# Zero fill of the expert slots: issued behind the first norm instead of behind the last gate unit

## The chip, the cores and the metric

The kernel runs on one core of one Trainium2 chip. The metric is device microseconds (us) from the first to the last instruction of one execution with what lies around it; less is better. The engines are named as the profile names them: PE (TensorE, matrix multiplies), DVE (VectorE), ACT (ScalarE), POOL (GpSimd) and SP (SyncE, which here only issues DMAs). All of them run at once and wait for each other through semaphores.

## What is computed

The reference is one inference step of a two-layer backbone over 640 tokens of 1024 channels, 128 context tokens and 512 latent ones. Each layer is a mixer and a mixture of experts, each behind a norm that is scaled and shifted:

```python
for l in range(DEPTH):                       # DEPTH = 2
    sh1, sc1, gt1, sh2, sc2, gt2 = ada_modulation(cvec, w_mod[l], b_mod[l])
    h = rmsnorm(x, norm_mix_g[l]) * (1.0 + sc1) + sh1
    y = mixer_ab(h, ...) if l % 2 == 0 else mixer_c(h, ...)
    x = x + gt1 * y
    h = rmsnorm(x, norm_ffn_g[l]) * (1.0 + sc2) + sh2
    x = x + gt2 * moe_ffn(h, router, bias, w1[l], w3[l], w2[l])
```

The mixer of layer 0 projects `h` to seven parts. Two feed a gated linear recurrence (RG-LRU: `xr`, `yr`, with gates from small block matrices), five feed a chunked recurrence with matrix states (HGRN2: `q`, two forget gates, `v`, `og`). In the mixture of experts each token goes to 2 of 16 experts:

```python
combine = jnp.sum(one_hot(idx, N_EXPERTS) * wsel[..., None], axis=1)   # 2 of 16 per token
hid = silu(einsum('md,edf->mef', hf, w1)) * einsum('md,edf->mef', hf, w3)
return einsum('mef,efd->md', hid * combine[..., None], w2)
```

## The kernel before, in words

Activations lie with channels on the 128 partitions, eight blocks of 128 channels by 640 tokens. The program of each engine is written out by hand in one block per engine; every engine takes its own list in order.

PE writes its results into a ring of four tiles in PSUM. `tile_plan` (function `T`) numbers all tiles in the order in which PE fills them; `psum_full` counts finished tiles, so a wait for `psum_full` at `T["name"] + n` is a wait until PE has finished the n-th tile of that name. Weights come through a ring of three slots of 1 MB. SP's `load_until` (line 568) issues the loads in a fixed order, and load i waits until PE has finished the last tile that uses load i − 3. PE waits for a load on `w_landed`.

Layer 0 begins on PE like this: transposes of the input, eight pieces of modulation (`mod0a`), the sums of the first norm (tile `norm0`), four `xr` and four `yr` projection tiles (two tiles for each 1 MB load of `ab_w_in`), and then eight units u = 0 to 7. A unit is two gate tiles (`gate`, from the small gate matrices `GW`) and one projection tile (`qk`). Behind each odd unit stand four further pieces of modulation (`mod0b`, one 1 MB load of `w_mod` each, 16 matmuls each) and a tile of transposes. Behind unit 7 follow the projections `kb`, `v` and `og`, and then the levels of the chunked recurrence. The norm's root is taken by ACT (lines 1399, 1400), the multiply by DVE (line 1789), scale and shift by ACT (line 1410), and `xr` starts on the first scaled blocks.

The mixture of experts sends tokens by their expert: a slot array in device memory, `slots_in` (`expert_inputs` in the trace), has 25 blocks of 128 rows, one for each of 16 experts and 9 for the overflow; `slots_out` (`expert_outputs`) has the same shape. Rows that no token fills are read too, so `slots_in` is filled with zeros, and so are the 9 overflow blocks of `slots_out`. The source is `ZERO`, 128 x 1024 zeros in SBUF, so each of the 34 fills moves 512 KB. POOL issues them in lines 723 to 726, and POOL waits for all of them (`zero_filled`) at the head of its part of the first mixture of experts, before it scatters tokens.

POOL's own list at the start is: small vectors, the gate matrices, the router, the memset of `ZERO`, then a wait for the second gate tile of unit 7 (`T["gate7"] + 2`). That wait protects `SIN`, the place of the recurrence's starting state, which lies in the second half of `GW`; the load of `state_hgrn` into it is issued next, and the 34 fills behind it. Then POOL takes its multiplies in the levels of the chunked recurrence (lines 737, 738).

Of the kernel before, what the change touches and what calls it, by code (L numbers as in the profile page):

```python
# [15 lines left out]
P = 128  # L16
# [149 lines left out]
def build(nc, A, const, outs, xspill, slots_in, slots_out):  # L166
# [6 lines left out]
    T = tile_plan()  # L173
    VB = vec_places()
    ctx = ExitStack()
    with ctx:  # L176
# [3 lines left out]
        def sem(name):  # L180
            return ctx.enter_context(nc.semaphore(name))
# [65 lines left out]
        psum_full = sem("psum_full")  # L247
# [91 lines left out]
        for i in range(4):  # L339
            add(("rw_wo", i), T["wo"] + 2 * i + 1, cols(A["rw_wo"][0], 256 * i, 256))  # L340
        slot_no = {key: i for i, (key, _, _) in enumerate(stream)}
        landed_at, per_slot = [], [0] * RING_W
        for i, (_, _, parts) in enumerate(stream):
            per_slot[i % RING_W] += 16 * len(parts)
            landed_at.append(per_slot[i % RING_W])
# [40 lines left out]
        SIN = GW[:, 8 * P:16 * P]  # L386
# [304 lines left out]
        def _(pool):  # L691
# [13 lines left out]
            for wi, name in enumerate(("rg_wa", "rg_wx")):  # L705
                for d in range(2):
                    src = A[name][0, d].rearrange("(c b) i j -> b i c j", b=2)
                    for b in range(2):
# [7 lines left out]
            pool.dma_start(rbias, rb.to_broadcast([P, NE])).then_inc(S["router_in"], 16)  # L716
            nc.gpsimd.memset(ZERO, 0.0).then_inc(S["zero_ready"], 1)

            pool.wait_ge(psum_full, T["gate7"] + 2)
            pool.dma_start(SIN.rearrange("p (j v) -> p j v", v=P),  # L720
                           A["state_hgrn"][0, 0].rearrange("d h k v -> k (d h) v")).then_inc(S["st_in"], 16)
            pool.wait_ge(S["zero_ready"], 1)
            for e in range(NE + N_OVER):
                pool.dma_start(slots_in[e * P:(e + 1) * P, :], ZERO).then_inc(S["zero_filled"], 16)
            for e in range(NE, NE + N_OVER):
                pool.dma_start(slots_out[e * P:(e + 1) * P, :], ZERO).then_inc(S["zero_filled"], 16)

            for h in range(NH_A):
                for lv in range(LEVELS):
                    i = h * LEVELS + lv  # L730
                    s = 1 << lv
                    nb = NT // (2 * s)
                    ek = EK[i % 3].rearrange("p (n two s) -> p n two s", two=2, s=s)
                    kf = K[0][:, h, :].rearrange("p (n two s) -> p n two s", two=2, s=s)
                    kb = K[1][:, h, :].rearrange("p (n two s) -> p n two s", two=2, s=s)
                    pool.wait_ge(S["lvl_exp"], 2 * i + 2)
                    nc.gpsimd.tensor_tensor(ek[:, :, 0, :], ek[:, :, 0, :], kf[:, :, 0, :], ALU.mult)
                    nc.gpsimd.tensor_tensor(ek[:, :, 1, :], ek[:, :, 1, :], kb[:, :, 1, :],
                                            ALU.mult).then_inc(S["lvl_k"], 1)
# [1798 lines left out]
```

## Time and profile before

| | us |
|---|---|
| median of 3 runs | 2493.36 |
| lowest and highest of them | 2492.8, 2500.39 |
| profiled execution | 2489.1 |
| its span, first to last instruction | 2487.3 |
| PE busy in it | 2086.2 (84%) |
| DVE, ACT, POOL busy | 974.9, 701.6, 376.7 |
| mean granted clock of PE | 0.894 |

All rows further down are of the one profiled execution, and times in them count from the start of its span. Busy shares are means over many stages with different limits, so a stage is read by itself: by what its engines wait for, by the granted clock of PE (1.00 is full speed) and by the share of the 16 DMA engines and the GB/s that they move. For a DMA the trace gives the time at which an engine issued it and the time until it landed.

### The profile page before, as it was taken

What the parts mean: (1) busy time and instruction counts of PE and PEld (TensorE: products, weight loads), DVE (VectorE), ACT (ScalarE), POOL (GpSimd) and SP (SyncE); (2) the same over time, 40 slices, a digit from 0 to 9 for tenths busy, and PEclk for the clock granted to TensorE, in tenths of its full rate; (3) what the DMA queues carried; (4) which work ended last, traced back from release to release, by engine and by line L of the source; (5) the groups of instructions that cost most, each with busy time, mean ns of one, the idle gap of its engine ahead of it and who ended that gap; (6) DMA issues with size and microseconds to landing.
All of it is one profiled execution on the core that took longest, in us unless ns stands there. A gap on an engine that the chain in (4) does not pass through costs nothing. (4 is left out here: it accounts for less than half of the span.)

```text
span 2487.3 us, 35375 instructions
## 1 busy us (share of the span) xinstructions
PE 2086.2 (84%) x14628; PEld 1519.2 (61%) x14628; DVE 974.9 (39%) x2165; ACT 701.6 (28%) x1491; POOL 376.7 (15%) x870
## 2 busy tenths in 40 slices
PE   6999698777885999559998998888888879759993
PEld 3454365444544777335577887878877865647762
DVE  2236303566222111271124566665666551311104
ACT  1245213222121111130034555444544330301112
POOL 3000300333001000200013333133223300010001
PEclk9999899898995999779999898886888899679996
DMA  8134832333224899622122111211121221469963
GB/s 277 34 119 135 310 138 68 104 115 122 92 89 165 272 342 343 200 92 69 51 61 48 34 42 42 44 33 35 40 42 33 52 77 35 152 220 344 344 232 136
DMA packets 330272, 322.30 MB, mean 130 GB/s; under 512 B 119028, under 2 KB 299488, under 8 KB 329728
## 3 DMA queue, kind: packets, MB, share of 16 engines
q1 hardware_dynamic: 311200, 253.70, 33.0%
q0 software_dynamic: 17456, 60.55, 6.4%
q10 hardware_dynamic: 1456, 5.77, 0.6%
q8 instruction: 118, 1.93, 0.3%
q14 instruction: 42, 0.34, 0.0%
HBM read 252.86 MB, written 67.12 MB: 129 GB/s over the span
## 5 line engine op out<-in xcount | busy, mean ns | idle before, releaser
L831 PE MATMUL psum_ring<-arena 64*64 64x32 f32 (+6 forms) x4800 | 625.6, 316 | 62.7 <-DVE arena L2311 28.6
L831 PEld LDWEIGHTS psum_ring<-arena 64*64 64x64 f32 (+2 forms) x4800 | 464.8, 179 | 183.8 <-issue 105.3
L831 PE MATMUL psum_ring<-arena,weight_ring 128*128 128x128 f32 (+2 forms) x1680 | 346.2, 359 | 6.1 <-DVE arena L2105 3.4
L831 PEld LDWEIGHTS psum_ring<-arena,weight_ring 128*128 128x128 f32 x1680 | 239.2, 198 | 110.8 <-issue 102.8
L831 PE MATMUL psum_ring<-h_normed,weight_ring 128*128 128x512 f32 (+1 forms) x768 | 214.9, 442 | 11.4 <-ACT h_normed L1410 5.8
L831 PE MATMUL psum_ring<-weight_ring,arena 64*64 64x64 f32 (+4 forms) x1776 | 195.4, 292 | 17.1 <-DVE h_normed L2381 4.1
L831 PE MATMUL psum_ring<-weight_ring,small 128*2 128x256 f32 x768 | 178.2, 390 | 18.0 <-DMA weight_ring<-in_w_mod 17.6
L831 PEld LDWEIGHTS psum_ring<-weight_ring,arena 64*64 64x64 f32 (+2 forms) x1776 | 170.6, 173 | 34.3 <-issue 10.3
L831 PEld LDWEIGHTS psum_ring<-h_normed,weight_ring 128*128 128x128 f32 x768 | 119.4, 195 | 106.1 <-issue 100.4
L831 PEld LDWEIGHTS psum_ring<-weight_ring,small 128*2 128x2 f32 x768 | 64.0, 86 | 121.2 <-DMA weight_ring<-in_w_mod 18.7
L1912 DVE COPY arena<-psum_ring 128x1024 f32<-128x1024 f32 x36 | 44.1, 1225 | 180.7 <-PE psum_ring L915 180.6
L831 PE MATMUL psum_ring<-x_resid,weight_ring 128*128 128x512 f32 (+1 forms) x320 | 88.9, 440 | 25.7 <-DVE x_resid L2175 25.7
L1435 ACT ACTIVATE arena<-psum_ring 128x256 f32<-128x256 f32 x36 | 13.8, 383 | 324.0 <-PE psum_ring L831 324.0
L1920 DVE TENSOR_TENSOR arena<-arena,psum_ring 128x256 f32<-128x256 f32 x36 | 15.2, 422 | 229.5 <-ACT arena L1435 229.5
L915 PE MATMUL psum_ring<-consts,arena 128*128 128x128 f32 x360 | 54.1, 285 | 53.5 <-DMA arena<-expert_inputs 53.5
L915 PEld LDWEIGHTS psum_ring<-consts,arena 128*128 128x128 f32 x360 | 46.7, 149 | 74.2 <-DMA arena<-expert_inputs 53.7
L831 PEld LDWEIGHTS psum_ring<-x_resid,weight_ring 128*128 128x128 f32 x320 | 49.4, 194 | 65.1 <-issue 65.1
L752 POOL DMA_DIRECT2D expert_outputs<-arena x36 | 19.3, 537 | 444.7 <-ACT arena L1430 427.6
L1394 ACT ACTIVATE h_normed<-x_resid 128x640 f32<-128x640 f32 x40 | 28.7, 734 | 200.5 <-DVE x_resid L1808 194.5
L797 POOL COPY arena<-arena 32x256 f32<-32x256 f32 x20 | 12.1, 603 | 463.1 <-DMA arena<-expert_outputs 463.1
L806 POOL TENSOR_TENSOR arena<-arena 64x14 f32<-64x14 f32 (+6 forms) x280 | 78.3, 279 | 21.9
L804 POOL TENSOR_TENSOR arena<-arena 64x14 f32<-64x14 f32 (+6 forms) x280 | 76.2, 272 | 22.0
(384 smaller groups left out, 2799.2 us busy)
## 6 DMA issues: line engine op xcount, KB each, us to landing
arena<-in_moe_w SPq DMA_DIRECT2D x108, 1024.0 KB, 10.5
weight_ring<-in_w_mod SPq DMA_DIRECT2D x48, 1024.0 KB, 5.1
expert_outputs<-arena POOLq DMA_DIRECT2D x45, 512.0 KB, 7.8
arena<-expert_inputs SPq DMA_DIRECT2D x36, 512.0 KB, 7.5
weight_ring<-in_ab_w_in SPq DMA_DIRECT2D x14, 1024.0 KB, 5.0
expert_inputs<-arena POOLq DMA_DIRECT2D x25, 512.0 KB, 17.4
arena<-expert_outputs SPq DMA_DIRECT2D x80, 128.0 KB, 3.2
expert_outputs<-arena SPq DMA_DIRECT2D x26, 256.0 KB, 2.8
```

The costliest lines, as they stand in the source:

```text
L752: pool.dma_start(slots_out[e * P:(e + 1) * P, :], YB[e % 2]).then_inc(y_stored[e % 2], 16)
L797: link(nc.gpsimd.tensor_copy(square(triL[0:NB_T]), turned(triX[0:NB_T])))
L804: link(nc.gpsimd.tensor_tensor(prod, l3[:, k + 1:, k:k + 1].broadcast_to([2 * NB_T, m, k]), r3[:, k:k + 1, 0:k].broadcast_to([2 * NB_T, m, ...
L806: link(nc.gpsimd.tensor_tensor(r3[:, k + 1:, 0:k], r3[:, k + 1:, 0:k], prod, ALU.subtract))
L831: return nc.tensor.matmul(out, lhsT, rhs, start=start, stop=stop)
L915: ins = nc.tensor.transpose(ps[:, k * P:(k + 1) * P], src[:, k * P:(k + 1) * P], ident)
L1394: A_(H[:, k, :], X[:, k, :], ACT.Square).then_inc(S["sq_ready"], 1)
L1435: A_(SH[e % 2], ps[:, 0:DE], ACT.Silu).then_inc(S["silu_out"], 1)
L1912: free(nc.vector.tensor_copy(XGT[e % 2], ps), n)
L1920: free(TT(HM[e % 2], SH[e % 2], tile(n)[:, 512:512 + DE], ALU.mult), n)
```

## The change

The load of `state_hgrn` with its wait for `T["gate7"] + 2` moves from ahead of the 34 fills to behind them. The fills get a wait of their own, for the tile `norm0`, with which PE has finished the sums of the first norm. The wait for `zero_ready` (the memset of `ZERO`) stays with the fills. The number of DMAs, their sizes and the queue that they are issued on are as before.

```diff
@@ -716,15 +716,16 @@
             pool.dma_start(rbias, rb.to_broadcast([P, NE])).then_inc(S["router_in"], 16)
             nc.gpsimd.memset(ZERO, 0.0).then_inc(S["zero_ready"], 1)
 
-            pool.wait_ge(psum_full, T["gate7"] + 2)
-            pool.dma_start(SIN.rearrange("p (j v) -> p j v", v=P),
-                           A["state_hgrn"][0, 0].rearrange("d h k v -> k (d h) v")).then_inc(S["st_in"], 16)
             pool.wait_ge(S["zero_ready"], 1)
+            pool.wait_ge(psum_full, T["norm0"] + 1)
             for e in range(NE + N_OVER):
                 pool.dma_start(slots_in[e * P:(e + 1) * P, :], ZERO).then_inc(S["zero_filled"], 16)
             for e in range(NE, NE + N_OVER):
                 pool.dma_start(slots_out[e * P:(e + 1) * P, :], ZERO).then_inc(S["zero_filled"], 16)
 
+            pool.wait_ge(psum_full, T["gate7"] + 2)
+            pool.dma_start(SIN.rearrange("p (j v) -> p j v", v=P),
+                           A["state_hgrn"][0, 0].rearrange("d h k v -> k (d h) v")).then_inc(S["st_in"], 16)
             for h in range(NH_A):
                 for lv in range(LEVELS):
                     i = h * LEVELS + lv
```

POOL's list at this place before, with the semaphores that a row waits for (`in_state_hgrn` is the state, `expert_inputs` and `expert_outputs` are the two slot arrays):

```order
L717 MEMSET arena 128x1024
L720 DMA arena<-in_state_hgrn 128x8x128 [waits psum_full]
L724 DMA expert_inputs<-arena 128x1024 [waits zero_ready]
L724 DMA expert_inputs<-arena 128x1024 x24
L726 DMA expert_outputs<-arena 128x1024 x9
L737 ISA
L737 TENSOR_TENSOR h_normed<-h_normed,arena 128x320 [waits lvl_exp]
```

Here the wait for the gate tiles (`psum_full` in the row of L720) stands ahead of all the fills. POOL's list at the same place in the changed kernel, whose lines from there on are numbered anew:

```order
L717 MEMSET arena 128x1024
L722 DMA expert_inputs<-arena 128x1024 [waits psum_full,zero_ready]
L722 DMA expert_inputs<-arena 128x1024 x24
L724 DMA expert_outputs<-arena 128x1024 x9
L727 DMA arena<-in_state_hgrn 128x8x128 [waits psum_full]
L738 ISA
L738 TENSOR_TENSOR h_normed<-h_normed,arena 128x320 [waits lvl_exp]
```

The 34 fills have moved ahead of the state's load, behind an earlier wait (`psum_full` of `norm0`); the wait for the gate tiles now holds the state's load alone. The lists of the other engines, SP's weight loads among them, are the same in both kernels.

## Rows read from the trace of the kernel before

**Rows 1.** The page's slices of 62.2 us: memory traffic.
```profile
GB/s 277 34 119 135 310 138 68 104 115 122 92 89 165 272 342 343 200 92 69 51 61 48 34 42 42 44 33 35 40 42 33 52 77 35 152 220 344 344 232 136
```

**Rows 2.** Waits of PE, 274.2 to 330 us: total, times, longest.
```profile
PE psum_ring L831 <- DMA weight_ring<-in_w_mod: 17.6, 2, 11.7
```

**Rows 3.** Timeline of PE, 274.2 to 330 us: start, length, group, idle time before it.
```profile
274.26 7.07 PE L831 MATMUL psum_ring<-weight_ring,small 128*2 128x256 f32 x32
293.00 5.77 PE L831 MATMUL psum_ring<-weight_ring,small 128*2 128x256 f32 x16 [11.67 <-DMA weight_ring<-in_w_mod]
304.76 5.03 PE L831 MATMUL psum_ring<-weight_ring,small 128*2 128x256 f32 x16 [5.98 <-DMA weight_ring<-in_w_mod]
...
316.54 13.84 PE L831 MATMUL psum_ring<-h_normed,weight_ring 128*128 128x512 f32 x41 [5.60 <-DMA weight_ring<-in_ab_w_in]
```

**Rows 4.** Timeline of PE, 230 to 256 us, behind unit 5.
```profile
237.37 13.97 PE L831 MATMUL psum_ring<-weight_ring,small 128*2 128x256 f32 x64
...
252.44 2.43 PE L831 MATMUL psum_ring<-arena 128*128 128x512 f32 x8
```

**Rows 5.** Timeline of POOL, 15 to 290 us, and line 726.
```profile
265.98 0.90 POOL L720 DMA_DIRECT2D arena<-in_state_hgrn  x1 [243.91 <-PE psum_ring L831]
266.87 13.24 POOL L724 DMA_DIRECT2D expert_inputs<-arena  x25
...
L726 POOL DMA_DIRECT2D expert_outputs<-arena x9: 532/532/534, 280.1 to 284.3; - x9
...
DMA to landing us min/median/max: 31.6/36.0/40.7
```

**Rows 6.** Weight loads of line 568, issued 270 to 282 us.
```profile
L568 SPq DMA_DIRECT2D weight_ring<-in_w_mod x2: 368/368/368, 274.4 to 277.9; - x2
L568 SPq DMA_DIRECT2D weight_ring<-in_ab_w_in x1: 8818/8818/8818, 281.4 to 281.4; - x1
...
DMA to landing us min/median/max: 18.6/26.8/35.1
```

**Rows 7.** Weight loads of line 568, issued 90 to 110 us.
```profile
L568 SPq DMA_DIRECT2D weight_ring<-in_ab_w_in x2: 368/368/368, 90.1 to 107.4; - x2
...
DMA to landing us min/median/max: 4.9/4.9/5.0
```

**Rows 8.** Windows: length, busy time (instructions) by engine, granted clock, DMA share, GB/s.
```profile
270.00:281.00 11.00, 11.00 (x49) 4.87 (x47) 8.56 (x7) 6.63 (x8) 11.00 (x22) 1.00 1.02 398
281.00:293.00 12.00, 0.33 (x3) 0.00 (x1) 2.55 (x6) 0.09 (x1) 3.82 (x8) 0.61 1.04 410
322.00:420.00 98.00, 98.00 (x397) 65.93 (x396) 14.96 (x16) 19.45 (x26) 0.00 (x0) 1.00 0.22 74
```

**Rows 9.** Timeline of ACT, 60 to 145 and 320 to 340 us.
```profile
63.95 0.77 ACT L1399 ACTIVATE psum_ring<-psum_ring,consts 128x640 f32<-128x640 f32 x1 [30.38 <-PE psum_ring L831]
...
124.76 0.70 ACT L1466 ACTIVATE arena<-psum_ring 128x640 f32<-128x640 f32 x1 [7.95 <-PE psum_ring L831]
...
142.07 0.70 ACT L1466 ACTIVATE arena<-psum_ring 128x640 f32<-128x640 f32 x1 [7.95 <-PE psum_ring L831]
...
327.82 0.70 ACT L1491 ACTIVATE arena<-psum_ring 128x640 f32<-128x640 f32 x1 [46.74 <-PE psum_ring L831]
...
336.48 0.70 ACT L1491 ACTIVATE arena<-psum_ring 128x640 f32<-128x640 f32 x1 [7.36 <-PE psum_ring L831]
```

**Rows 10.** Timeline of PE, 62 to 146 us.
```profile
69.67 72.36 PE L831 MATMUL psum_ring<-h_normed,weight_ring 128*128 128x512 f32 x256 [5.76 <-ACT h_normed L1410]
141.87 2.33 PE L831 MATMUL psum_ring<-arena 128*128 128x512 f32 x8
```

**Rows 11.** Timeline of DVE: 62 to 75, 232 to 246, 267 to 283 us.
```profile
66.75 5.68 DVE L1789 TENSOR_TENSOR h_normed<-x_resid,psum_ring 128x1280 f32<-128x1280 f32 x4 [5.97 <-ACT psum_ring L1400]
...
236.75 4.15 DVE L2022 RECIPROCAL arena<-arena 128x640 f32<-128x640 f32 x1
...
272.69 4.15 DVE L2022 RECIPROCAL arena<-arena 128x640 f32<-128x640 f32 x1
```

## The prediction

> **What bounds the kernel now.** The page first: the chain of work at its end is spread over PE, ACT, DVE and DMA, so no single engine's share says what this edit is worth. The slices of the page do: where the edit works, in the fifth slice (249 to 311 us), the core moves 310 GB/s while its neighbours move 135 and 138 [rows 1]. Next, what PE waits for there. Between 274 and 330 us its longest are for weight loads, 17.6 us in two waits for `w_mod` [rows 2]. The timeline of PE puts them in order and adds a third: the four `w_mod` pieces behind unit 7 start at 274.26, stall until 293.00 and again until 304.76, and the next projection (`kb`) starts at 316.54, 5.60 us of that a wait for `ab_w_in` [rows 3]. The same stretch of unit 5, with no fill beside it, goes from 237.37 to 252.44 [rows 4]. POOL's timeline names the culprit: 34 fills of 512 KB (25 to `expert_inputs`, 9 to `expert_outputs`) are issued from 266.87, one each 0.53 us, the last at 284.3, and it lands 40.7 us later, at 325.0 [rows 5]. Weight loads issued beside them at 274.4, 277.9 and 281.4 take 18.6, 26.8 and 35.1 us to land [rows 6]; undisturbed ones take 4.9 to 5.0 [rows 7]. They land at 293.0, 304.7 and 316.5, exactly where PE resumes, 11.8 us apart. So this stretch is bound by DMA bandwidth: the windows show the engines at a share of 1.04 and 410 GB/s while PE works 0.33 us of 12 [rows 8]. ACT and DVE only wait for PE there.
>
> **The change part by part.** *(a) The fills leave 266.87 to 325.0.* The weight loads then take 5 us as behind units 1, 3 and 5. The loads issued at 274.4 and 277.9 would land at 279.4 and 282.9, before PE comes to them at 281.2 and 284.7 (two and three pieces of 13.97/4 = 3.49 us behind 274.26 [rows 4]), the one of 281.4 at 286.4, before `kb` at 289.3. The stretch shrinks from 316.54 − 274.26 = 42.28 us to unit 5's 252.44 − 237.37 = 15.07: **27.2 us saved**, waits and half-speed pieces together.
>
> *(b) The clock behind the stall.* PE is idle from 281, the granted clock falls to a mean of 0.61 in 281 to 293 (1.00 is 2.4 GHz, the lower level is 1.2) [rows 8], and the idle stretches before 304.76 and 316.54 repeat it. The first projection of `kb` takes from 316.54 until ACT reads it at 327.82: 11.28 us. Its neighbour takes 336.48 − 327.82 = 8.66 [rows 9], plus 0.20 from PE's next start to ACT's read (141.87 and 142.07 [rows 9, 10]). **2.4 us saved**: with no idle time PE keeps 2.4 GHz, as it does behind unit 5.
>
> *(c) Who is late next.* From 322 to 420 PE is busy 98.00 us of 98 at clock 1.00 [rows 8] with the `kb`, `v` and `og` projections; ACT and DVE wait for PE's tiles, POOL for ACT's exponents. Nothing there has a fixed time, so the whole path moves up. The state load keeps its wait on the last gate unit (265.98 [rows 5]) and now has an empty queue behind it; its reader comes over 100 us later. Cost: nothing.
>
> *(d) The fills arrive behind the first norm.* POOL has been idle since 22 us; it is released when PE ends the sums of `norm0`, 63.95 by ACT's read [rows 9], plus the 0.3 us it took at 265.98. The 34 issues take 18 us on POOL, which nobody waits for. The data: 34 x 0.524 MB = 17.8 MB at 398 to 410 GB/s [rows 8] is 45 us alone, 58.1 us in the old place (266.87 to 325.0) with about four weight loads sharing. Here two loads share, so about 53 us, bounds 45 and 58: it ends near 117 us (109 to 122.4). In the whole of 64 to 125 us SP issues only two loads, at 90.1 and 107.4 [rows 7]. The first belongs to `yr` tile 2, which starts when `yr` tile 1 is done, at 124.6 (ACT's read at 124.76 [rows 9]); the second is needed behind the gate tiles of 141.87 [rows 10]. With 18.6 us (a first load beside the fill [rows 6]) they land at 108.7 and 126.0: 16 us to spare each. With the worst landing seen, 35.1, they are at 125.2 and 142.5, under 1 us late. With the fill ahead of everything until 122.4, the first lands at 127.3, 2.7 us late. Cost 0, bounds 0 and 3; I take 0, because the nearest row, one load in flight beside the fill, is 18.6.
>
> *(e) The fill beside PE, DVE and ACT.* In 270 to 281, with the fill at 398 GB/s, PE is busy 11.00 of 11.00 us at clock 1.00 [rows 8]; DVE's reciprocal takes 4.15 us beside POOL's issues (272.69) and 4.15 without (236.75) [rows 11]. Cost 0. The cover is gone only if the norm's chain on DVE and ACT (64 to 70 us), for which PE waits 5.76 us [rows 10], is different; that is rival 1.
>
> **Sum**: 27.2 + 2.4 = 29.6 us off the profiled execution's 2489.1 (span 2487.3): 2459.5. The median of the runs is 2493.4, 4.3 above it, and the forecast of a median is 2493.4 − 29.6 = **2463.8 us**.
>
> **Rivals.** *1. POOL's burst holds DVE.* The first multiplies of the norm (DVE, 66.75 to 72.4 [rows 11]) would lie inside POOL's 18 us of issues (64.3 to 82.4). If DVE had to wait for the burst's end, PE's first projection would move by 82.4 − 66.75 = 15.6 us: 2479.4. Against it: the equal reciprocals of (e). A page bears on this. The Trainium skill, "SBUF — State Buffer", section "SBUF: two separate sides", says that VectorE and GpSimd share a pair of ports as an exclusive lock, held for a whole instruction, and that a DMA issued from GpSimd needs it to write its descriptors; it limits this to VectorE's two-port modes and to some operations with two SBUF inputs. By that rule the burst might be late as well as DVE; the rows show neither, and the norm's multiply has one operand in PSUM.
>
> *2. The clock does not come back.* If the pieces ran as slowly as beside the stall, only the waits are saved, 11.67 + 5.98 + 5.60 = 23.2 us [rows 3]: 2470.2. Against it: unit 5 has equal work before it, and its pieces take 13.97 us.
>
> *3. The loads were slow for another reason, or the fill does not start early:* 2493. For it speaks only that the profile infers releasers; against it the landing times, which hold to the fill's end. POOL's queue holds nothing ahead of the fills after 22 us.
>
> *4. Slower: the fill outlasts its room.* Place: `yr` tile 2 at 124.6, waiting for the load issued at 90.1. If weight loads got nothing until the fill ends, and it ran slower than in the old place, PE would wait; the gain is used up when that load lands later than 124.6 + 29.6 = 154.2, so when 17.8 MB take from 66 to 149 us, 215 GB/s or less. At the 135 GB/s of the slice ahead of the old place [rows 1] the fill takes 132 us and ends at 198, the load lands at 203, and PE loses 78 us: 2493.4 − 29.6 + 78 = 2542. Against it: the same bytes on the same queue moved at 400 GB/s, and loads beside it did get 1 MB each 11.8 us.
>
> **How the numbers follow.** Forecast 0.88; rival 1: 0.03; rival 2: 0.04; rival 3: 0.03; rival 4: 0.02. A measurement of this kernel tells 0.3% (7.5 us) from no change. Faster holds the forecast and rivals 1 and 2: 0.95; same is rival 3: 0.03; slower 0.02. The range: the runs before lie from 2489.1 to 2500.4, so −4 and +7 about the median; with the 29.6 taken off that is 2459.5 to 2470.8. Cost (d) of up to 3 and rival 2 (2470.2) widen the top to 2474. The two saved terms come from one neighbour each, and a stall less can also shift a later fall of the clock, whose size the spread of the runs gives as some 4 us: the bottom goes to 2455.
>
> **What would show it.** Right: POOL's fills start at about 64.3 us and the last lands between 109 and 122; PE runs from 69.7 to the gates without a wait; the loads of 90.1 and 107.4 land in some 19 us; PE goes from the last `w_mod` pieces at 274 to `kb` at 289, at clock 1.00; `kb`'s first read by ACT is near 298; everything from there is 29.6 us earlier. Wrong: a wait of PE for `in_ab_w_in` near 125, DVE's multiplies of the norm longer than 5.68 us, or new waits between 289 and 400 us that take the place of the old.

## The result

| | us | ratio to before, 95% interval |
|---|---|---|
| before, median of four runs | 2493.08 | |
| changed kernel, median of four runs (2460.35 to 2473.12) | 2465.27 | 0.9888 (0.9853 to 0.9923) |
| changed kernel, measured a second time, median | 2464.74 | 0.9868 (0.9840 to 0.9895) |
| profiled execution, before and after | 2489.1, 2460.35 | |
| its span, before and after | 2487.3, 2458.5 | |

Each ratio is to runs of the kernel before that were made beside it. The changed kernel is faster by 27.8 us by the medians; the forecast was a gain of 29.6 us, to a median of 2463.8. The second measurement was made beside the experiments:

> The changed kernel once more, on the chip of these runs, as the mark for the others: ratio 0.985 to 0.991.

**The stretch behind unit 7.** The timeline of PE in the changed kernel, 262 to 330 us, answers rows 3:

```profile
272.83 13.97 PE L832 MATMUL psum_ring<-weight_ring,small 128*2 128x256 f32 x64
287.32 0.65 PE L870 MATMUL psum_ring<-consts,arena 2*128 2x2 f32 x8 [0.51 <-DVE arena L1770]
287.90 34.88 PE L832 MATMUL psum_ring<-h_normed,weight_ring 128*128 128x512 f32 x128
```

The four `w_mod` pieces run in one block of 13.97 us and `kb` starts at 287.90, 15.07 us after the first of them, as behind unit 5 before [rows 4] and where the kernel before took 42.28. The weight loads issued there (line 568, 270 to 282 us; issue time, then landing) answer rows 6:

```profile
L568 SPq DMA_DIRECT2D weight_ring<-in_w_mod x2: 368/368/368, 272.9 to 276.5; - x2
L568 SPq DMA_DIRECT2D weight_ring<-in_ab_w_in x1: 367/367/367, 279.9 to 279.9; - x1
...
DMA to landing us min/median/max: 5.0/5.1/5.1
```

They land in 5 us in place of 18.6 to 35.1. (On the page the fifth slice of the span now moves 140 GB/s in place of 310 [rows 1], the second 325 in place of 34.) The waits of PE in the whole first 420 us (total, times, longest) are:

```profile
PE psum_ring L996 <- DMA arena<-in_rw_lnb: 17.5, 1, 17.5
PE psum_ring L832 <- POOL h_normed L739: 13.3, 1, 13.3
PE psum_ring L832 <- ACT h_normed L1411: 5.8, 1, 5.8
PE psum_ring L870 <- DVE arena L1770: 3.0, 6, 0.5
```

No wait for a load of `w_mod` or `ab_w_in` is left [rows 2], and none has come up elsewhere. The waits for `in_rw_lnb`, for the norm (line 1411) and for line 1770 were there before with the same 17.5, 5.8 and 3.0 us. The wait for POOL (13.3 us, line 739) is that of line 738 before, at the first level of the chunked recurrence; it had 13.32 us there and has only moved into the window.

**The fills in their new place.** POOL's timeline, 15 to 290 us, and the landing times of the last nine fills answer rows 5:

```profile
64.55 13.12 POOL L722 DMA_DIRECT2D expert_inputs<-arena  x25 [42.47 <-PE psum_ring L832]
77.67 4.72 POOL L724 DMA_DIRECT2D expert_outputs<-arena  x9
264.55 0.91 POOL L727 DMA_DIRECT2D arena<-in_state_hgrn  x1 [182.16 <-PE psum_ring L832]
...
L724 POOL DMA_DIRECT2D expert_outputs<-arena x9: 532/532/534, 77.7 to 81.9; - x9
...
DMA to landing us min/median/max: 26.7/29.9/34.4
```

They are issued from 64.55, the last at 81.9, and it lands 34.4 us later, at 116.3. The two weight loads issued meanwhile answer rows 7 (one window each):

```profile
L568 SPq DMA_DIRECT2D weight_ring<-in_ab_w_in x1: 368/368/368, 88.7 to 88.7; - x1
...
DMA to landing us min/median/max: 18.3/18.3/18.3
...
L568 SPq DMA_DIRECT2D weight_ring<-in_ab_w_in x1: 368/368/368, 106.0 to 106.0; - x1
...
DMA to landing us min/median/max: 11.6/11.6/11.6
```

They land at 107.0 and 117.6; PE comes to the first at about 123.1 (0.20 us ahead of ACT's read at 123.33) and to the second behind 140.44. The windows (columns as in rows 8) and PE's timeline from 62 to 146 us [rows 10]:

```profile
70.00:82.00 12.00, 12.00 (x40) 6.48 (x40) 3.57 (x5) 8.06 (x14) 12.00 (x24) 0.89 1.02 374
82.00:109.00 27.00, 27.00 (x102) 15.05 (x101) 10.12 (x21) 3.93 (x4) 0.39 (x1) 1.00 1.03 401
281.00:293.00 12.00, 11.49 (x53) 5.59 (x52) 2.36 (x7) 0.00 (x0) 0.00 (x0) 1.00 0.81 264
```

```profile
69.70 70.90 PE L832 MATMUL psum_ring<-h_normed,weight_ring 128*128 128x512 f32 x256 [5.76 <-ACT h_normed L1411]
140.44 2.33 PE L832 MATMUL psum_ring<-arena 128*128 128x512 f32 x8
```

With the DMA engines at 374 and 401 GB/s PE is busy in every microsecond of 70 to 109, and the 5.76 us that it waits for the norm are the same to the digit [rows 10]. DVE's multiplies of the norm and ACT's reads of `yr` tile 1 and of the first `kb` tile [rows 9, 11]:

```profile
66.77 5.68 DVE L1790 TENSOR_TENSOR h_normed<-x_resid,psum_ring 128x1280 f32<-128x1280 f32 x4 [5.98 <-ACT psum_ring L1401]
```

```profile
123.33 0.70 ACT L1467 ACTIVATE arena<-psum_ring 128x640 f32<-128x640 f32 x1 [7.95 <-PE psum_ring L832]
...
296.85 0.70 ACT L1492 ACTIVATE arena<-psum_ring 128x640 f32<-128x640 f32 x1 [17.19 <-PE psum_ring L832]
```

The multiplies take 5.68 us beside POOL's burst as they did without it. `kb` is read at 296.85, 30.97 us earlier than at 327.82.

### The profile page after: what moved, and what is told of

The parts are those of the page before. It is cut to its first block and busy times, and to the rows that moved or that the text cites. A ratio compares the mean times of both kernels' runs of the same rounds, so it can differ in the third digit from the quotient of the medians.

```text
span 2458.5 us, 35376 instructions
## 1 busy us (share of the span) xinstructions
PE 2080.5 (85%) x14628; PEld 1518.0 (62%) x14628; DVE 975.0 (40%) x2165; ACT 701.4 (29%) x1491; POOL 377.6 (15%) x870
## 3 DMA queue, kind: packets, MB, share of 16 engines
q10 hardware_dynamic: 1456, 5.77, 0.6%
## 5 line engine op out<-in xcount | busy, mean ns | idle before, releaser
L832 PE MATMUL psum_ring<-weight_ring,arena 64*64 64x64 f32 (+4 forms) x1776 | 196.1, 294 | 16.9 <-DVE h_normed L2382 4.1
L832 PEld LDWEIGHTS psum_ring<-h_normed,weight_ring 128*128 128x128 f32 x768 | 117.6, 192 | 98.5 <-issue 98.4
```

The costliest lines, as they stand in the source:

```text
L832: return nc.tensor.matmul(out, lhsT, rhs, start=start, stop=stop)
```

## Experiments

One theory stood against several rivals from the start. Theory A: the fills take DMA bandwidth from weight loads, and what it costs depends on which loads are issued beside the fill and how soon PE needs them. Its rivals put the gain down to the order in POOL's queue (B), to being early as such (C, E), or to the bytes as such (D). A mark that all runs share is ACT's read of the first `kb` tile: 327.82 before, 296.85 and 298.24 in two profiles of the changed kernel.

### The order alone

```diff
-            pool.wait_ge(psum_full, T["norm0"] + 1)
+            pool.wait_ge(psum_full, T["gate7"] + 2)
```

The edit is to the changed kernel: the state's load stays behind the fills, but both wait for the last gate unit.

> The order of POOL's queue alone: the 34 fills stand ahead of the state load, as in the changed kernel, but both still wait for the last gate unit. Theory A (the fills take DMA bandwidth from the weight loads behind unit 7): no gain, ratio to the kernel before 1.000 +- 0.003, PE again waits some 23 us for loads and the first kb read by ACT is near 328 us. Theory B (the state load ahead of the fills held something back, the order is what counts): ratio 0.988 to 0.99, kb read near 298.

Measured: 2494.28 us, ratio 1.0007 (0.9986 to 1.0028), `kb` read at 326.43. The waits of PE, 250 to 330 us:

```profile
PE psum_ring L832 <- DMA weight_ring<-in_w_mod: 18.0, 2, 11.7
PE psum_ring L832 <- DMA weight_ring<-in_ab_w_in: 4.3, 1, 4.3
```

The stall is there in full, 18.0 + 4.3 us, with loads landing after 18.6, 26.7 and 35.0 us. The order of the queue is worth nothing; it is the time of the fills. Theory B falls.

### Other places

The wait of the fills was moved to three further places. First, without any wait, so that they start at 22.43 us:

```diff
-            pool.wait_ge(psum_full, T["norm0"] + 1)
```

> The fills without any wait for PE, so they start near 22 us, beside the input and the first eight w_mod loads. Theory A: the loads fall from 5 us apiece to 11.8 us apiece while the fill runs (about 55 us), four to five of them do, PE waits 25 to 30 us for w_mod ahead of the first norm, and the gain behind unit 7 is used up: ratio 0.997 to 1.004, first norm's sums done near 90 us in place of 64. Theory C (the earlier the fill the better, only the place behind unit 7 is bad): ratio 0.988.

Measured: 2502.66 us, ratio 1.0029 (1.0010 to 1.0048). The waits of PE, 20 to 110 us, and its timeline around the sums of the first norm:

```profile
PE psum_ring L831 <- DMA weight_ring<-in_w_mod: 27.8, 6, 8.5
```

```profile
81.09 5.15 PE L831 MATMUL psum_ring<-weight_ring,small 128*2 128x256 f32 x16 [5.90 <-DMA weight_ring<-in_w_mod]
86.41 3.62 PE L831 MATMUL psum_ring<-weight_ring,small 128*2 128x256 f32 x16 [0.17 <-DMA weight_ring<-in_w_mod]
...
91.11 8.92 PE L831 MATMUL psum_ring<-h_normed,consts 128*128 128x512 f32 x32
```

PE waits 27.8 us for `w_mod`, as forecast, but the sums of the norm end near 100.0 in place of 64, 36 us late and not 26: the pieces between the waits run at the lower clock too (5.15 us for 16 matmuls at 81.09, 3.49 undisturbed). The stretch behind unit 7 is clean here, and still `kb` is read at 334.34, 6.5 us later than before, and the kernel is slower than before by 0.3%. Being early is no gain by itself, theory C falls.

Second, behind the last `yr` tile:

```diff
-            pool.wait_ge(psum_full, T["norm0"] + 1)
+            pool.wait_ge(psum_full, T["yr"] + 4)
```

> The fills 77 us later, behind the last yr tile (141 us), so that they lie under the first four w_mod pieces of the units in place of the last four. Theory A (what counts is which loads are issued beside the fill and how soon PE needs them): the loads issued from 162 us land late, PE waits 15 to 22 us between 169 and 200, ratio 0.996 to 1.000. Theory C (anywhere ahead of unit 7 is free): ratio 0.989.

Measured: 2490.41 us, ratio 0.9980 (0.9966 to 0.9994), `kb` read at 319.13. PE's timeline, 150 to 205 us:

```profile
162.85 7.07 PE L832 MATMUL psum_ring<-weight_ring,small 128*2 128x256 f32 x32
181.03 6.39 PE L832 MATMUL psum_ring<-weight_ring,small 128*2 128x256 f32 x16 [11.11 <-DMA weight_ring<-in_w_mod]
192.77 5.65 PE L832 MATMUL psum_ring<-weight_ring,small 128*2 128x256 f32 x16 [5.35 <-DMA weight_ring<-in_w_mod]
```

The stall of the kernel before has moved to the pieces behind unit 1 (11.11 and 5.35 us, and slow pieces with it), where loads of the same kind are issued as closely ahead of their need. Of the 31 us at the mark 8.7 are left.

Third, later than in the kernel before, behind the first `kb` tile (an edit to the kernel before, so the state's load goes first):

```diff
             pool.wait_ge(S["zero_ready"], 1)
+            pool.wait_ge(psum_full, T["kb"] + 1)
```

> The fills later than in the kernel before, behind the first kb tile (about 297 us). Theory A: in the 105 us from there PE has long projections and each load is issued 17 us or more ahead of its need; the load issued near 305 takes some 19 us and is needed at 322.6, so PE waits 0 to 2 us: ratio 0.988 to 0.990, as good as behind the first norm. Theory E (the fill must be early): ratio 1.00 or above.

Measured: 2471.44 us, ratio 0.9902 (0.9880 to 0.9925). The changed kernel measured beside it has 0.9868 (0.9840 to 0.9895): this run is 6.7 us longer by the medians of four runs each, the intervals overlap, and the times alone do not tell whether the place is quite as good. The load issued beside the fill, and PE's timeline, 280 to 400 us:

```profile
L568 SPq DMA_DIRECT2D weight_ring<-in_ab_w_in x1: 367/367/367, 306.4 to 306.4; - x1
...
DMA to landing us min/median/max: 18.1/18.1/18.1
```

```profile
288.83 34.88 PE L832 MATMUL psum_ring<-h_normed,weight_ring 128*128 128x512 f32 x128
324.66 34.77 PE L832 MATMUL psum_ring<-weight_ring,h_normed 128*128 128x256 f32 x160 [0.95 <-issue]
359.27 34.77 PE L832 MATMUL psum_ring<-h_normed,weight_ring 128*128 128x512 f32 x128
```

The load lands at 324.5 and PE waits 0.95 us for it (the profile calls this wait "issue"). What follows PE's last projection starts at 393.88, against 391.76 and 393.15 in the two profiles of the changed kernel. So up to there a place 234 us later is as good to within a microsecond or two, and theory E falls too. With four places tried, two are free and two cost 22 and 37 us at the mark (`kb` read at 319.13 and 334.34 in place of 296.85), and what differs between them in the traces is how soon PE needs the loads that are issued beside the fill.

### Fewer and more bytes

Nine fills (4.7 MB) were left behind the last gate unit, the other 25 put behind the norm (an edit to the changed kernel):

```diff
-            for e in range(NE, NE + N_OVER):
-                pool.dma_start(slots_out[e * P:(e + 1) * P, :], ZERO).then_inc(S["zero_filled"], 16)
 ...
             pool.wait_ge(psum_full, T["gate7"] + 2)
+            for e in range(NE, NE + N_OVER):
+                pool.dma_start(slots_out[e * P:(e + 1) * P, :], ZERO).then_inc(S["zero_filled"], 16)
```

> Dose: 25 fills behind the first norm, the 9 fills of the output slots still behind the last gate unit. Theory A with a threshold: 9 fills are 4.7 MB, 11.6 us at 407 GB/s, and are nearly through when the loads issued at 273 and 277 are needed, so PE waits about 3 us: 3 us above the changed kernel, ratio 0.990, kb read by ACT near 300. Theory D (each fill behind unit 7 costs its 34th of 29.6 us): 7.8 us above the changed kernel, ratio 0.992, kb read near 305.

Measured: 2474.66 us, ratio 0.9913 (0.9881 to 0.9944), `kb` read at 305.49. PE's timeline, 262 to 335 us, and the landing of the load that it waits for:

```profile
273.89 7.07 PE L831 MATMUL psum_ring<-weight_ring,small 128*2 128x256 f32 x32
287.02 8.43 PE L831 MATMUL psum_ring<-weight_ring,small 128*2 128x256 f32 x32 [6.07 <-DMA weight_ring<-in_w_mod]
...
296.54 34.88 PE L831 MATMUL psum_ring<-h_normed,weight_ring 128*128 128x512 f32 x128
```

```profile
L568 SPq DMA_DIRECT2D weight_ring<-in_w_mod x1: 368/368/368, 274.0 to 274.0; - x1
...
DMA to landing us min/median/max: 13.0/13.0/13.0
```

Theory A had 3 us for this and the runs show 6.07 of waiting and 1.5 of slow pieces: 296.54 − 273.89 = 22.65 in place of 15.07. The number 7.6 is that of theory D (7.8), so this run does not tell the two apart; the next one does. Its trace shows where the time goes: into one wait, for the first load issued behind the fills, which takes 13.0 us although the last fill lands at 282.4; after it PE runs on. What was wrong in the expectation is the size: the load lands 4.6 us after the last fill, where it had been expected nearly with it. The state's load, 512 KB more, stands behind the nine fills in POOL's queue and lands at 284.6; the expectation had left it out. How much of the 4.6 us it makes is not shown.

The other way, 16 more fills behind the norm (the blocks of `slots_out` that nothing needs filled):

```diff
-            for e in range(NE, NE + N_OVER):
+            for e in range(NE + N_OVER):
                 pool.dma_start(slots_out[e * P:(e + 1) * P, :], ZERO).then_inc(S["zero_filled"], 16)
 ...
-                pool.wait_ge(S["zero_filled"], 16 * (NE + 2 * N_OVER))
+                pool.wait_ge(S["zero_filled"], 16 * 2 * (NE + N_OVER))
```

> Room behind the first norm: 50 fills in place of 34 are issued there (the 16 other blocks of the output slots are filled too, which no one needs). The fill then ends near 138 us in place of 115. Theory A: the loads issued at 89, 106 and 123 us have 16 us or more to spare with 12 to 19 us of landing, so nothing is late: the time of the changed kernel, ratio 0.988, no wait of PE for a load ahead of 285 us. Rival (the bytes cost wherever they move, 29.6 us for 34 fills): 16 more cost 14 us, ratio 0.994.

Measured: 2469.96 us, ratio 0.9899 (0.9861 to 0.9936). The three loads beside the fill land in 18.3, 16.7 and 16.4 us, PE waits for none of them, and `kb` is read at 297.44, between the two profiles of the changed kernel (296.85 and 298.24):

```profile
297.44 0.70 ACT L1492 ACTIVATE arena<-psum_ring 128x640 f32<-128x640 f32 x1 [17.20 <-PE psum_ring L832]
```

8.4 MB more cost nothing at the mark, where theory D had 14 us for them, and its ratio of 0.994 lies outside the interval. So theory D falls: a fill costs by what waits behind it.

### The clock by itself

The second term of the sum, 2.4 us, was taken apart from the first: in the kernel before, matmuls of no use (their tile is overwritten) fill PE's waits behind unit 7, so that the loads stay late but the clock stays up.

```diff
+            def spin(ps, n):
+                for _ in range(n):
+                    mm(ps[0:2, 0:256], silu_c[:, 0:2], H[:, 0, 0:256])
 ...
+                ps = open_tile(n)
+                spin(ps, {22: 26, 23: 17}.get(i, 0) if layer == 0 else 0)
                 w = weights(("mod", layer, i))
-                ps = open_tile(n)
 ...
+                ps = open_tile(n)
+                spin(ps, 16 if n == T["kb"] else 0)
                 w = weights(key, c)
-                ps = open_tile(n)
```

A first run had 54, 30 and 26 of them:

> The kernel before, with matmuls of no use (their tile is overwritten) put where PE waits behind unit 7: 54 ahead of the third w_mod piece, 30 ahead of the fourth, 26 ahead of the first kb tile, so that PE stays at its higher clock through the waits for loads. Theory A, the two terms of the sum: the loads still land at 293, 305 and 316.5, kb still starts near 316.5 (the stall stays), but its first tile takes 8.9 us to ACT's read in place of 11.3: read near 325.4, 2.4 us off the whole. Rival (the slow clock is part of what delays kb's start): kb starts at 311 or earlier.

It missed: each took 0.435 us, twice what was assumed, PE was still at them when the loads had landed, `kb` started at 335.41 and the run took 2520.09 us, so it tells nothing of the stall. Of the clock's price it does: at clock 1.00 the first `kb` tile took 344.37 − 335.41 = 8.96 us to its read. The second run has about half as many:

> The run before with the number of useless matmuls mended: in it each took 0.435 us, twice what was assumed, so PE was late for loads that had landed. Now 26, 17 and 16 of them, 11.3, 7.4 and 7.0 us. Theory A: the last loads land near 305 and 316.5 as in the kernel before, kb starts at 316 to 317, its first tile takes 8.9 us to ACT's read: read near 325.4, against 327.8 before and near 297 in the changed kernel. Rival (without the fall of the clock the stall itself is shorter): kb starts at 312 or earlier.

Measured: 2490.52 us in one run. PE's timeline, 262 to 350 us, its windows, and ACT's read:

```profile
279.63 11.39 PE L831 MATMUL psum_ring<-h_normed,small 128*2 128x256 f32 x52
...
294.55 7.50 PE L831 MATMUL psum_ring<-h_normed,small 128*2 128x256 f32 x34
302.71 3.61 PE L831 MATMUL psum_ring<-weight_ring,small 128*2 128x256 f32 x16 [0.66 <-DMA weight_ring<-in_w_mod]
...
314.47 34.88 PE L831 MATMUL psum_ring<-h_normed,weight_ring 128*128 128x512 f32 x128
```

```profile
281.00:293.00 12.00, 11.92 (x56) 4.53 (x55) 1.07 (x3) 0.00 (x0) 2.28 (x5) 1.00 1.04 409
293.00:316.00 23.00, 21.83 (x103) 8.79 (x102) 1.17 (x4) 0.00 (x0) 0.00 (x0) 1.00 1.04 413
316.00:322.00 6.00, 6.00 (x23) 3.28 (x22) 0.00 (x0) 0.00 (x0) 0.00 (x0) 1.00 1.04 407
```

```profile
323.43 0.70 ACT L1497 ACTIVATE arena<-psum_ring 128x640 f32<-128x640 f32 x1 [43.88 <-PE psum_ring L831]
```

In the kernel before, the first microseconds of `kb` ran at a granted clock of 0.56:

```profile
316.50:322.00 5.50, 5.46 (x11) 2.88 (x12) 0.00 (x0) 0.00 (x0) 0.00 (x0) 0.56 1.04 410
```

Here the clock is 1.00 throughout, the DMA engines are as full as before (1.04), and the load of `kb`, issued at 279.8, lands 34.6 us later, at 314.4, where PE starts. The stretch from the first piece to `kb` is 314.47 − 272.73 = 41.7 us, 0.5 less than the 42.28 before; the first `kb` tile takes 8.96 us to its read in place of 11.28. The third and fourth piece ran at full speed (3.62 and 3.61 us in place of 5.77 and 5.03), and still the stretch is hardly shorter, for the load of `kb` ends it. So the two terms are separate: the clock is worth 2.3 us here, and the 27 us are the loads'. The whole run's time is one run and says less than these marks.

## Why the prediction was right

Of the sum, step by step, at the mark of ACT's read of `kb`:

| step | forecast | measured |
|---|---|---|
| (a) stretch behind unit 7, 42.28 us before | 15.07, 27.2 saved | 15.07, 27.21 saved |
| (b) first `kb` tile to its read, 11.28 before | 8.86, 2.4 saved | 8.95, 2.33 saved |
| (c) what comes next | moves up whole | no new wait up to 392 |
| (d) fills behind the norm, end of the fill | 0, at 117 | 0, at 116.3 |
| (d) landing of the two loads | 18.6 each | 18.3 and 11.6 |
| (e) PE, DVE, ACT beside the fill | 0 | 0 |
| not in the sum: projections ahead of the gates | | 1.43 saved |
| together | 29.6 | 30.97 |

The 1.43 us come from PE's first projections: the granted clock of 70 to 82 us has a mean of 0.89 where it was 0.77 before, so that the gates start at 140.44 and not at 141.87. It is not the fill's doing: with a fill in this stretch the gates start at 140.44, 141.03, 141.49 and 141.84 in four profiles, without one at 140.33, 140.38, 141.01, 141.12, 141.37 and 141.87 in six. In the changed kernel's second profile, where they start at 141.84, `kb` is read 29.58 us earlier than before, which is the forecast.

At the matmul that follows PE's last projection, 422.73 before and 391.76 after, the whole 30.97 us still stand. From there to the end it is 2064.6 and 2066.7 us, so that 28.8 us are left between the spans. This rest is longer or shorter from profile to profile (2064.6 to 2082.5 over eleven), and the fills' place is not seen in it: with fills behind unit 7 or later it is 2064.6 to 2078.9, with all of them earlier 2066.7 to 2082.5. In the longest of them, the run with 50 fills, the page's line of PE and the granted clock show where the time lies, beside those of the changed kernel:

```profile
PE 2098.3 (85%) x14628; PEld 1533.5 (62%) x14628; DVE 974.8 (39%) x2165; ACT 701.7 (28%) x1491; POOL 383.5 (15%) x886
...
core 0: 2474.9 us, clock 0.889
```

```profile
PE 2080.5 (85%) x14628; PEld 1518.0 (62%) x14628; DVE 975.0 (40%) x2165; ACT 701.4 (29%) x1491; POOL 377.6 (15%) x870
...
core 0: 2458.5 us, clock 0.896
```

The same 14628 matmuls keep PE busy 17.8 us longer (16.9 of them in this rest) at a mean clock of 0.889 against 0.896. The five runs with 50 fills lie from 2464.07 to 2476.7 us in the order of their clocks, 0.894 to 0.889. What makes the clock differ from run to run was not seen. The forecast's range had taken this swing from the spread of the runs. That the profiled 2460.35 lies only 0.9 above the forecast of 2459.5 is in part luck: 1.43 us won ahead of the gates and 2.2 lost in the rest, neither of them by the edit, nearly cancel.

The rivals: DVE was not held by POOL's burst (5.68 us both times), the clock came back (b), the loads were slow for no other reason (a, and the run with the order alone), and the fill did not outlast its room, not even with 50 fills. The lock on a shared pair of ports of which the Trainium skill tells ("SBUF — State Buffer", section "SBUF: two separate sides") shows in no row here: beside the burst the multiplies took 5.68 us and the 34 issues 0.532 to 0.553 us each.

One reading of the prediction was too simple. It took 18.6 us for the landing of either load beside the fill. A load with next to no other load ahead of it took 16.4 to 18.8 us wherever the fill ran on until it landed, the first one (18.0 to 18.6 in nine profiles) and later ones alike (16.7 and 16.4 with 50 fills, 18.8 for the load issued at 323.7 in the run behind `kb`). A load issued towards the fill's end is quicker: the second one took 11.6 here, 7 us less than forecast, and 10.4 in the second profile. The prediction also counted two loads between 64 and 125 us where a third was issued at 124.8. Neither changed the sum, because PE needed none of these loads before it had landed.

No version faster than the changed kernel came out of these runs. In the two free places the fills cost PE a microsecond or nothing up to the end of the projections, so there is little left to gain by moving them.

## What to carry to other kernels

A bulk transfer that nobody waits for still has a price, and it is paid by the loads that are issued beside it: look for a stretch in which the next loads are needed later than they would land beside the transfer (here the first takes 13 us longer than undisturbed and still lands 16 us early), and release the transfer there. Early or late by itself decides nothing: starts at 64.55 and 298.36 us were free, starts at 22.43, 141.90 and 266.87 were not. To price the stall, compare the stretch with an undisturbed repeat of itself in the same trace, from the same first to the same next instruction; that takes in waits and lower clock together, and came out to 0.1 us here. Check the gain at a mark close behind the edit, because the rest of a long program can swing by more than the error of the sum.

## What the runs showed of the hardware

Beside a stream of 512 KB stores from POOL's queue (374 to 413 GB/s in all), a 1 MB load from SP's queue with next to no other load ahead of it landed 16.4 to 18.8 us after issue as long as the stream lasted, and loads issued close behind it landed 11.7 us after each other, against 5.0 undisturbed. That is 5 to 7 us more for a load by itself than the steady 11.7; it was not seen what the load does in that time. And PE's granted clock stayed at 1.00 through a stall of 30 us that was filled with matmuls of no use, at no cost to the loads (34.6 us to landing against 35.1), in the one execution that was run.
